# A conditioned hybrid decoder layer on one core: the sparse indexer taken head by head and earlier, projection tiles in another order, the output gate on the projected result, and one-instruction search candidates

## What is computed

```python
mod = silu(c) @ ada_w + ada_b                       # shift, scale, gate
h = rmsnorm(x, norm_g) * (1 + scale) + shift
z = h @ w_in                                        # 2760 columns
xr, gr, q, k, v, ga, qi, ki, wi = split(z)
xr = causal_depthwise_conv(xr, conv_w, conv_b)      # 512 channels, 4 taps
y_r = rg_lru(xr, ...) * silu(gr)                    # recurrence over positions
# sparse attention, 8 query heads, one shared key and value head
score[t, s] = sum_h relu(qi[t, h] . ki[s] / 8) * wi[t, h] / sqrt(8)   # 8 indexer heads
idx = top_k(score, 256)                             # causal
y_a = attention(q, k, v over idx) * silu(ga)
y = concat([y_r, y_a]) @ w_out
x = x + gate * y
out = rmsnorm(x, final_g)
```

## Time and profile before

| what | value |
|---|---|
| time before, median of 3 runs | 681.26 us (681.05 to 681.62) |
| time of the profiled execution | 682.19 us |
| its span | 680.4 us |
| PE busy | 557.4 us (82%) |
| VectorE (DVE) busy | 450.7 us (66%) |
| ScalarE (ACT) busy | 386.6 us (57%) |
| GpSimd (POOL) busy | 244.6 us (36%) |
| mean granted clock of TensorE | 0.902 |

### The profile page before, as it was taken

One profiled execution on the slowest core, in us unless ns is written; L12 is line 12 of the kernel. 1 busy time (PEld: TensorE's weight loads), 2 busy tenths in 40 slices (PEclk: granted clock), 3 DMA queues, 4 the chain that ended last, 5 costly groups with the idle time before them and its releaser, 6 DMA issues.

```text
span 680.4 us, 8136 instructions
## 1 busy us (share of the span) xinstructions
PE 557.4 (82%) x2704; PEld 453.4 (67%) x2704; DVE 450.7 (66%) x1021; ACT 386.6 (57%) x693; POOL 244.6 (36%) x201
## 2 busy tenths in 40 slices
PE   2379999888799369491799997276999999999995
PEld 2356888656678247181676885266889998888874
DVE  5984000877995998959699796467566666655631
ACT  6423122585459589496789365343465666666631
POOL 5042656063425353445472553454120202022121
PEclk9759999998999779596799999555999999999999
DMA  8940446200101011026112322800201001010111
GB/s 341 409 118 1 120 129 145 72 31 0 32 1 51 11 32 31 3 82 255 32 32 62 92 65 63 285 24 1 93 16 47 30 34 53 11 63 30 35 62 63
DMA packets 15450, 51.98 MB, mean 76 GB/s; under 512 B 3888, under 2 KB 3888, under 8 KB 14384
## 3 DMA queue, kind: packets, MB, share of 16 engines
q1 hardware_dynamic: 15408, 51.45, 23.5%
HBM read 37.81 MB, written 4.19 MB: 62 GB/s over the span
## 4 chain that ended last, share of the span: by engine, by line
PE 51%; DVE 19%; ACT 12%; issue 8%; DMA 5%; POOL 2%; SPq 2%; DVEq 0%; POOLq 0%; ACTq 0%
PE pair L1272 16%; PE pair L1381 13%; PE pair L1403 6%; PE pair L1414 5%; DMA ada<-in_ada_w 4%; ACT bias_sb L779 3%; DVE bias_sb L1013 3%; PE pair L1359 3%; PE pair L1360 2%; PE pair L1266 2%; PE pair L1423 2%; DVE score_sb L1130 2%; DVE tinies L1029 1%; DVE rnn_xc L1102 1%; ACT relu L793 1%
## 5 line engine op out<-in xcount | busy, mean ns | idle before, releaser
L1272 PE MATMUL pair<-h_hi,w_hi 128*128 128x512 f32 (+1 forms) x352 | 113.4, 404 | 20.8 <-ACT raw L756 17.7
L1272 PE MATMUL pair<-h_hi,w_lo 128*128 128x512 f32 (+1 forms) x352 | 110.3, 395 | 0.0
L1272 PE MATMUL pair<-h_lo,w_hi 128*128 128x512 f32 (+1 forms) x352 | 110.1, 394 | 0.0
L779 ACT ACTIVATE bias_sb<-score_sb,tinies 128x1024 bf16<-128x1024 f32 (+2 forms) x93 | 95.7, 1031 | 21.2 <-DVE tinies L1029 21.1
L1203 DVE TENSOR_TENSOR pt_lo<-pair,pt_hi 128x512 fp32r<-128x512 f32 (+3 forms) x96 | 50.5, 554 | 64.7 <-ACT pt_hi L884 64.3
L1272 PEld LDWEIGHTS pair<-h_hi,w_hi 128*128 128x128 f32 (+1 forms) x352 | 65.5, 190 | 38.1 <-issue 24.3
L1272 PEld LDWEIGHTS pair<-h_lo,w_hi 128*128 128x128 f32 (+1 forms) x352 | 66.3, 188 | 15.5 <-issue 0.8
L1272 PEld LDWEIGHTS pair<-h_hi,w_lo 128*128 128x128 f32 (+1 forms) x352 | 66.2, 188 | 15.2 <-issue 0.4
L1013 DVE TENSOR_SCALAR_CACHE_REDUCE bias_sb<-score_sb,tinies 128x640 bf16<-128x640 f32 (+2 forms) x93 | 74.0, 796 | 0.0
L884 ACT ACTIVATE pt_hi<-pair 128x512 fp32r<-128x512 f32 (+3 forms) x96 | 43.6, 489 | 27.6 <-PE pair L1414 25.3
L591 POOL TENSOR_SCALAR w_hi<-w_raw 128x1024 fp32r<-128x1024 f32 (+1 forms) x22 | 25.7, 1166 | 89.9 <-PE pair L1272 74.0
(11 more groups left out here) (200 smaller groups left out, 1378.4 us busy)
## 6 DMA issues: line engine op xcount, KB each, us to landing
w_raw<-in_w_tiles SPq DMA_DIRECT2D x21, 512.0 KB, 3.9
ada<-in_ada_w SPq DMA_DIRECT2D x8, 1024.0 KB, 18.9
x_sb<-in_x SPq DMA_DIRECT2D x8, 512.0 KB, 7.6
qs<-half_hi SPq DMA_DIRECT2D x16, 256.0 KB, 3.6
qs<-half_lo SPq DMA_DIRECT2D x16, 256.0 KB, 4.4
ada_g<-in_ada_w SPq DMA_DIRECT2D x1, 4096.0 KB, 13.7
wo_raw<-in_w_out SPq DMA_DIRECT2D x8, 512.0 KB, 7.4
x_res<-in_x SPq DMA_DIRECT2D x8, 512.0 KB, 3.3
```

The costliest lines, as they stand in the source:

```text
L779: nc.scalar.activation(junk[i], score_sb[:, SCORE_OFF[i]:SCORE_OFF[i] + keys_of(i)], ACT.Sign, bias=cand[:, c:c + 1], scale=-1.0, accum_ou ...
L1272: ins = nc.tensor.matmul(psum[banks[half]][0:width, :], w[b][:, k, 0:width], hh[:, k, half * HALF:(half + 1) * HALF], start=(k == 0 and p ...
```

## The change

1. **Tile order.** `gate`, `kv` and the four `q` now stand before all four `ga`.
2. **Indexer head by head.** `UNITS` has the head outermost, and the planner spreads the 48 units over the four tiles `qi` 2, `qi` 3, `xr` 0 and `gr` 0 (two heads a tile) instead of 20 k-steps from the last one of `xr` 0. All causal masks and sign counts now come behind the last unit.
3. **The planner** charges search rounds with the VectorE and ScalarE work that falls into them, and puts them into the list accordingly.
4. **Search candidates.** `cand = (miss ^ bit/2) ^ cand` in one instruction that reads the old candidate as a scalar operand; `spare` and its instruction go.
5. **Output gate.** `w_out` is no longer multiplied by the gate. VectorE multiplies the projected result (`yg`), GpSimd adds it to the residual, for the last block VectorE does both. The output pieces start at step 20 instead of 17, two a step up to step 26; the rounding of `w_out` is in steps 5 to 12.
6. **Loads and waits.** `ada_g` is loaded when the last unit has left PE; `final_g` goes into the free part of `qs` when 16 attention steps are done. PE waits for the last evacuation only ahead of its first transposes.

The core of the diff:

```diff
-TILES += [("ga", _ct, P) for _ct in range(3)]
-TILES += [("kv", 0, P), ("gate", 0, P)] + [("q", p, P) for p in range(4)] + [("ga", 3, P)]
+TILES += [("gate", 0, P), ("kv", 0, P)] + [("q", p, P) for p in range(4)] + [("ga", p, P) for p in range(4)]
-UNITS = [(i, h) for a, b in PAIRS for h in range(NH) for i in (a, b)]
+UNITS = [(i, h) for h in range(NH) for a, b in PAIRS for i in (a, b)]
-OUT_START = 17
+WO_START = 5
+OUT_START = 20
...
+        n = j - J["qi", 2]
+        if 0 <= n < 4:
+            for _ in range(HEAD_UNITS * (k + 1) // KC - HEAD_UNITS * k // KC):
+                w = keys_of(UNITS[units][0])
+                at(now, "idx", units, dve=0.2 + w / 900, act=0.2 + w / 1200)
...
+    t = start
     for it in range(SEARCH_BITS):
-        at(start + 4.0 + ROUND_US * it, "count", it)
+        at(t, "count", it)
+        end = t + ROUND_US
+        for _ in range(3):
+            d, a = (sum(x[n] for x in load if t <= x[0] < end) for n in (1, 2))
+            end = t + ROUND_US + max(d, a)
+        t = end
...
-                if kind == "ga" and n == 1:
-                    sp.wait_ge(slot_done, len(SLOT))
+                if kind == "xr" and n == 1:
+                    sp.wait_ge(slot_done, IDX_SLOTS)
                     sp.dma_start(ada_g[:, :, :], ...).then_inc(adag_in, 16)
+                if kind == "gate":
                     sp.wait_ge(rnn_done, CT)
                     sp.dma_start(gate_b[:, :], ...)
...
+                    for half in range(2):
+                        pool.wait_ge(y_ok, 2 * ti + half + 1)
+                        xs = x_res[ti % 2][...]
+                        nc.gpsimd.tensor_tensor(xs, yg[half], xs, ALU.add).then_inc(x1_ok, 1)
...
                 def take(c):
                     dve.wait_ge(count_a, ACT_COLS * it + c + 1)
-                    nc.vector.tensor_scalar(cols(c, hit), cols(c, cnt), cols(c, lim), float(bit), ALU.is_le, ALU.mult).then_inc(hit_ok, 1)
-                def narrow(c, hits):
-                    dve.wait_ge(hit_ok, 4 * it + hits)
-                    nc.vector.tensor_tensor(icand[:, c:c + 1], cols(c, hit), cols(c, spare[it % 2]), ALU.bitwise_xor).then_inc(cand_a, 1)
+                    nc.vector.tensor_scalar(cols(c, miss), cols(c, cnt), cols(c, lim), float(bit), ALU.is_gt, ALU.mult).then_inc(miss_ok, 1)
+                def narrow(c, misses):
+                    dve.wait_ge(miss_ok, 4 * it + misses)
+                    nc.vector.tensor_scalar(icand[:, c:c + 1], cols(c, miss), bit >> 1, icand[:, c:c + 1],
+                                            ALU.bitwise_xor, ALU.bitwise_xor).then_inc(cand_a, 1)
...
-                if it < SEARCH_BITS - 1:
-                    nc.vector.scalar_tensor_tensor(spare[1 - it % 2][:, :], hit[:, :], flip, spare[it % 2][:, :], ALU.bitwise_xor, ALU.bitwise_xor).then_inc(spare_ok, 1)
...
-                if g % 2 == 0 and g < 16:
-                    nc.vector.tensor_tensor(wo_raw[:, m, :], wo_raw[:, m, :], gate_bc[:, :], ALU.mult).then_inc(wo_scaled, 1)
-                if g % 2 == 1 and g < 16:
+                if WO_START <= g < WO_START + KC:
                     nc.vector.tensor_scalar(wo_hi[:, m, :], wo_raw[:, m, :], 1.0, None, ALU.mult).then_inc(wo_hi_ok, 1)
...
-                    nc.vector.tensor_tensor(xs, bank(3), xs, ALU.add).then_inc(x1_ok, 1)
+                    nc.vector.tensor_tensor(yg[half], bank(3), gate_bc[...], ALU.mult).then_inc(y_ok, 1)
+                    if ti == NT - 1:
+                        nc.vector.tensor_tensor(xs, yg[half], xs, ALU.add).then_inc(x1_last, 1)
```

More of the change, by code:

```diff
@@ L115, in stages, with at @@
     due = []
-    def at(us, *what):
+    load = []
+    def at(us, *what, dve=0.0, act=0.0):
         due.append((us, len(due), what))
-    ks = [(j, k) for j in range(J["xr", 0], NJ) for k in range(KC)]
+        load.append((us, dve, act))
+    ks = [(j, k) for j in range(J["qi", 1], NJ) for k in range(KC)]
     now = 0.0
@@ L124, in stages @@
     rnn_us = 0.0
-    for n, (j, k) in enumerate(ks):
+    start = 0.0
+    for j, k in ks:
         kind, ct, _ = TILES[j]
@@ L141, in stages @@
         now += 1.72 if kind == "gate" else 1.365
+        n = j - J["qi", 2]
[3 more added lines that the diff above has]
+                at(now, "idx", units, dve=0.2 + w / 900, act=0.2 + w / 1200)
+                now += 2 * w / 2400 + 0.06
+                units += 1
+            if units == len(UNITS) and not start:
+                at(now + 2.0, "causal")
+                for c in range(len(PICK)):
+                    at(now + 3.0, "nonneg", c, dve=0.9)
+                at(now + 4.0, "bias01")
+                at(now + 8.0, "prep", dve=3.0)
+                at(now + 9.0, "sign", act=3.0)
+                start = now + 12.0
         if k == KC - 1:
             us = now + 0.2
-            if kind == "ga" and ct == 0:
+            if kind not in ("qi", "xr", "gr"):
                 us = max(us, rnn_us)
-            at(us, "evac", j)
+            if (kind, ct) == ("q", 0):
+                us += 2 * 1.365
+            at(us, "evac", j, act={"xr": 1.1, "gr": 1.1, "gate": 1.1, "kv": 3.1}.get(kind, 2.1))
             if j in SLAB and SLAB[j] + 2 < NW:
@@ L191 @@
             SLOT[_o + (_g,)] = len(SLOT)
+IDX_SLOTS = max(SLOT["idx", u] for u in range(len(UNITS))) + 1
 def pt_ring():
@@ L1282, in _ @@
                 kstep(1, k)
-            for k in range(3):
-                kstep(2, k)
             pe.wait_ge(evac_done, 1)
```

146 lines of the change are left out of this document (70 added, 76 removed).

## The result

The changed kernel takes **693.11 us** (692.06 to 693.34, 4 runs), against 681.44 (681.05 to 681.62, 4 runs) for the kernel before in the same comparison: ratio 1.0169, interval [1.0151, 1.0187]. It is 11.7 us slower. I had forecast 677.7, and 667 to 690 as the range.

A forecast was written before the change was run, and what follows sets the result against it. Bound by the recurrence chain with search rounds from 200 to 327 us, by PE in the attention proper. Terms +1.0 - 7.5 + 2.2 + 0.7 = -3.6 against the median 681.26 gave 677.7 us, range 667 to 690.

The forecast's parts named there:

- Start of the recurrence: Indexer ahead of the recurrence: last index sum 34.5 us earlier, at 162.5, but `gr` 1 still evacuated at 200.5.
- The recurrence: From `gr` 1 to `gate`: 23.5 us a channel tile without rounds, 31 with two; `gate` evacuated at 292.3.
- Rival B: Longer passage to step 0: 34 us a channel tile, masks at 26, `gate` later than 296; 688 us, chance 0.25.
- To the end of the projections: Eight tiles on PE after `gate`, 87.5 us plus 2.9 for low clock; projections end at 384.9 against 422.2.
- The exposed end: Behind the last projection tile: evacuation, five rounds, settling and masks, 49.7 us; step 0 at 435.0, +1.0.
- Search candidates at 0.1: New candidate instructions in the search rounds: at worst 0.1 us exposed in each of 14 rounds, 1.4 us.
- Steps 0 to 15, -7.5: Early attention steps: eight gate products go, saving 7.5 us (3 to 10); 34 us instead of 41.6.
- Steps 16 to 26, +2.2: Attention with later output pieces: PE no longer full in steps 17 to 19, costing 2.2 us (0.5 to 7).
- tail, +0.7: End of the kernel: VectorE does product and addition one after the other, costing 0.7 us (0.5 to 1).
- Rival C: Attention gives nothing: steps 0 to 15 gain 3, low clock in steps 17 to 19 costs 7; 684 us, chance 0.12.
- Rival A: Rounds cost nothing inside the recurrence: a channel tile takes 27 us, step 0 moves by 11; 667 us, chance 0.18.
- the signs named beforehand: Wrong if `gate` is off over 4 us, PE stalls in the last eight tiles, or steps 0 to 15 take 40.

The follow-up runs named there:

- e9: The kernel before with all 31 search rounds moved behind the recurrence: 681.62 us, ratio 1.0000.
- e3: The changed kernel with no search round ahead of the recurrence's last scan, and rounds every 3.1 us instead of 4.0 behind it: 684.33 us, ratio 1.003.
- e1: The changed kernel with GpSimd's split of the next weight slab moved behind the recurrence's third product: 686.54 us, ratio to the kernel before 1.0066.
- e5: The kernel before with the new search candidates alone: 677.11 us, ratio 0.9929.
- e12: The changed kernel with the old search candidates (XOR of two tiles, spare candidate kept): 694.25 us, ratio to the kernel before 1.0192.
- e7: The changed kernel with the casts of w_out at the odd steps 1 to 15, as before: 688.53 us, ratio to the kernel before 1.0097.
- e8: The changed kernel with the output projection's pieces from step 17 instead of 20: 690.93 us, ratio to the kernel before 1.0138.

## Why the prediction was wrong

By its own steps, in order, with the changed profile:

- *Start of the recurrence.* Last index sum forecast at 162.5, measured to end at 163.1; `gr` 1 at 200.5, measured 203.28. Right to 2.8 us.
- *The recurrence: "23.5 a channel tile" and "I take 31".* **This is the term that failed.** It measured 36.1, and `gate` came at 303.66 instead of 292.3, +11.4. The 23.5 came from taking six rounds at 3.08 each out of 42; taking them out of that kernel left 30.1 (e9). The two remaining rounds cost what I added for them, 3.1 each (e3): 29.8 + 6.3 = 36.1. So the failed part is the tile without rounds, 24.8 in my walk (31 less 6.2) and 29.8 measured. Of the 5.0 too much, 3.0 are the weight split that the new list puts in front of the product (e1) and that my walk left out. The other 2.0 no run separates. The way to `gate` adds up: 2.8 up to `gr` 1, 2 x 5.0 for the two tiles, and 1.5 less than forecast from `gr` 3 to `gate` (28.3 for 29.8).
- *Rival B* named this: "34 a channel tile", and that it decides from a `gate` later than 296. It gave 688. Its condition was met and its direction came out; it was 5 us short. Its masks at 26 did not come.
- *To the end of the projections.* 92.6 us forecast from `gate`'s evacuation, 90.7 measured. Right.
- *The exposed end.* 49.7 forecast, 47.2 from the last evacuation to step 0. The masks took 23.3 from the first comparison (418.34) to step 0, 23.6 forecast; L1085's twin L1114 took 1.28, forecast 1.33 (1.02 in proportion is 1.36). Right. The errors so far sum to the 6.6 us by which step 0 came late (441.60 for 435.0).
- *Search candidates at 0.1.* Mis-sized: worth 4.7 us in the kernel before (e5); in the changed one about 1 (e12), which isn't clear of the noise.
- *Steps 0 to 15, -7.5.* Measured -1.1. The chain without the products does take 35.5 (e7), but the eight casts came to stand at successive steps, where six of them wait for GpSimd's subtraction.
- *Steps 16 to 26, +2.2, and tail, +0.7.* Together +4.7 instead of +2.9. The tail, from the last projection piece of the last step to the end, is 0.8 longer (24.35 and 23.54 by the chain), so the late pieces cost 3.9; 2.7 of it goes with `OUT_START = 17` (e8). GpSimd's additions took 1.30 us each (1.4 forecast) and held nobody up.
- *Rival C's clock.* The granted clock was 1.00 in the 24 us behind step 16, with PE 91% busy: the emptier steps didn't lower it. That the attention gave nothing, as C is titled (+3.6 in all, -1.1 and +4.7), had other causes. C's own terms (+1.0, -3, +7, +0.7) also sum to 687, not to 684. *Rival A* is refuted: rounds aren't free in the recurrence.
- Of the signs named beforehand two came: `gate` off by 11.4, and steps 0 to 15 still at 40.5. PE had next to no stalls in the last eight tiles (89.56 of 90.73 us busy).
